# Block 2's odd steps: the weight split behind the gate banks and the lag rows

## What is computed

```
h = rms_norm(x, norm_gain[layer])
proj = h @ w_in[layer]
q, k, v, z_a, u, z_s, g_a, g_s = jnp.split(proj, SPLITS, axis=-1)
y_a = band_attention(heads(q), heads(k), heads(v), rel_bias[layer])
y_a = (y_a * jax.nn.silu(z_a)) @ w_attn_out[layer]
y_s = s5_ssm(u, ...)
y_s = jax.nn.gelu(y_s)
glu_a, glu_b = jnp.split(y_s @ w_glu[layer] + b_glu[layer], 2, axis=-1)
y_s = glu_a * jax.nn.sigmoid(glu_b)
y_s = (y_s * jax.nn.silu(z_s)) @ w_ssm_out[layer]
merged = jax.nn.sigmoid(g_a) * y_a + jax.nn.sigmoid(g_s) * y_s
x = x + merged @ w_out[layer]
```

## Time and profile before

| | |
|---|---|
| median of the runs | 1469.31 us |
| profiled execution, its own time | 1469.46 us |
| its span in the profile | 1467.6 us |
| granted TensorE clock, mean | 0.999 |
| TensorE busy | 1374.2 us (94%) |
| VectorE busy | 546.7 us (37%) |
| ScalarE busy | 339.7 us (23%) |
| GpSimd busy | 115.3 us (8%) |

### The profile page before, as it was taken

One profiled execution on the slowest core, in us unless ns is written; L12 is line 12 of the kernel. 1 busy time (PEld: TensorE's weight loads), 2 busy tenths in 40 slices (PEclk: granted clock), 3 DMA queues, 4 the chain that ended last, 5 costly groups with the idle time before them and its releaser, 6 DMA issues.

```text
span 1467.6 us, 16657 instructions
## 1 busy us (share of the span) xinstructions
PE 1374.2 (94%) x6713; PEld 737.4 (50%) x6713; DVE 546.7 (37%) x965; ACT 339.7 (23%) x549; POOL 115.3 (8%) x190
## 2 busy tenths in 40 slices
PE   7999999999998898998988988989899999999997
PEld 6778433333333232332332323324378787888876
DVE  7675621121211121121111211213268587756663
ACT  5893110010000000010000000103042465533322
POOL 0000000000000000000000000002022214550000
PEclk9999999999999999999999999999999999999999
DMA  9149899999999999999999999999975133253231
GB/s 324 22 172 385 324 420 406 428 427 428 429 429 430 429 430 430 429 429 429 430 429 429 429 429 428 428 428 428 404 245 139 58 101 86 83 171 134 92 110 58
DMA packets 67827, 467.31 MB, mean 318 GB/s; under 512 B 5760, under 2 KB 30592, under 8 KB 42688
## 3 DMA queue, kind: packets, MB, share of 16 engines
q1 hardware_dynamic: 62864, 454.71, 75.4%
q0 software_dynamic: 4624, 11.44, 3.1%
q10 hardware_dynamic: 288, 0.45, 0.1%
HBM read 458.49 MB, written 7.05 MB: 317 GB/s over the span
## 4 chain that ended last, share of the span: by engine, by line
PE 62%; DMA 30%; DVE 4%; ACT 2%; issue 2%; DVEq 0%; POOL 0%; ACTq 0%
DMA wide<-in_w_up 22%; PE bank L1028 13%; PE bank L970 12%; PE bank L724 8%; PE bank L726 8%; PE bank L725 8%; DMA early<-in_w_up 8%; PE bank L911 4%; PE bank L998 1%; PE bank L1066 1%; DVE nrm L1746 1%; PE bank L1125 1%; PE bank L1153 1%; PE bank L754 1%; PE bank L764 0%
## 5 line engine op out<-in xcount | busy, mean ns | idle before, releaser
L970 PE MATMUL bank<-wide,xinT 128*64 128x512 f32 x1376 | 307.2, 596 | 43.2 <-DMA wide<-in_w_up 24.6
L970 PEld LDWEIGHTS bank<-wide,xinT 128*64 128x64 f32 x1376 | 96.5, 137 | 249.7 <-issue 170.5
L970 PE MATMUL bank<-early,xinT 128*64 128x512 f32 x656 | 147.2, 596 | 19.8 <-DMA early<-in_w_up 11.1
L1746 DVE SCALAR_TENSOR_TENSOR th<-th,bank 128x512 f32<-128x512 f32 x32 | 20.6, 684 | 387.8 <-ACT th L1451 387.8
L1028 PE MATMUL bank<-wide,actT 128*64 128x512 f32 x656 | 145.1, 595 | 3.6 <-issue 3.4
L724 PE MATMUL bank<-hT_lo,ring_r 128*128 128x512 f32 x352 | 138.6, 394 | 1.4 <-ACT gt L1316 1.1
L726 PE MATMUL bank<-hT_hi,ring_r 128*128 128x512 f32 x352 | 137.1, 389 | 0.0
L725 PE MATMUL bank<-hT_hi,ring_r 128*128 128x512 f32 x352 | 137.0, 389 | 0.0
L1451 ACT ACTIVATE th<-bank 128x512 f32<-128x512 f32 x32 | 17.4, 595 | 477.1 <-PE bank L970 477.1
L1743 DVE TENSOR_TENSOR ring_r<-ring,ring_r 128x2048 fp32r<-128x2048 f32 (+1 forms) x40 | 89.4, 2236 | 59.9 <-ACT ring_r L1284 59.4
L970 PEld LDWEIGHTS bank<-early,xinT 128*64 128x64 f32 x656 | 45.9, 137 | 119.2 <-issue 79.1
(11 more groups left out here) (427 smaller groups left out, 1705.4 us busy)
## 6 DMA issues: line engine op xcount, KB each, us to landing
wide<-in_w_gate SPq DMA_DIRECT2D x43, 2048.0 KB, 37.7
wide<-in_w_up SPq DMA_DIRECT2D x42, 2048.0 KB, 39.0
wide<-in_w_down SPq DMA_DIRECT2D x39, 2048.0 KB, 38.5
early<-in_w_down SPq DMA_DIRECT2D x21, 2048.0 KB, 38.5
early<-in_w_up SPq DMA_DIRECT2D x21, 2048.0 KB, 39.0
early<-in_w_gate SPq DMA_DIRECT2D x20, 2048.0 KB, 40.1
ring<-in_w_in SPq DMA_DIRECT2D x25, 1024.0 KB, 6.2
ring<-in_w_out SPq DMA_DIRECT2D x8, 1024.0 KB, 4.9
```

The source lines that it names most:

```text
L970: last = pe.matmul(bank[1 + 2 * (m % 2) + q // 2][o:o + 64, :], xinT[:, k, :], w[:, i, q * 512:(q + 1) * 512], start=(k == 0), stop=(k == ...
L1746: return dve.scalar_tensor_tensor(out_, a, s, b, op0, op1)
```

## The change

In the odd steps 1, 3, 5 and 7 VectorE calls `weights_lo(M + 9 + i)` behind the gates' evictions and the lag rows instead of ahead of them. Nothing is added or removed, and the programs of the other engines are the same.

```diff
                 if i % 2 == 1 and i < HEADS:
                     states(i // 2)
-                weights_lo(M + 9 + i)
+                late = i % 2 == 1 and i < HEADS
+                if not late:
+                    weights_lo(M + 9 + i)
                 if i == HEADS:
...
-                if i % 2 == 1 and i < HEADS:
+                if late:
                     c = i // 2
                     lag_rows(c)
+                    weights_lo(M + 9 + i)
                     if c + 1 < CT:
                         full(dve, f"st_im_{c}")
                         input_table(c + 1)
```

## The result

The changed kernel takes 1477.23 us (median of 6 runs, 1476.0 to 1478.43) against 1469.73 us for the kernel before (6 runs). The ratio is 1.0051, with a 95% interval of 1.0038 to 1.0064: slower by 7.5 us. The forecast was 1473.9 us, with a range to 1475.5. The direction was right; of the 7.5 us the forecast's sum had 4.6.

The account below looks back on a forecast made before the run. TensorE's products were taken to bound block 2, so other engines count only where TensorE waits. Terms -0.84 + 0.58 + 1.49 + 1.68 + 1.67 = +4.58 us gave 1473.9 us, range 1472.0 to 1475.5.

Parts of the forecast that it names:

- The wait in step 3 goes, -0.84: TensorE's wait before step 3's lag product, for a gate bank VectorE has not yet emptied, goes whole: -0.84 us.
- Room of 1.8 us for the split in steps 1, 3 and 5, 0.58 us too little in step 7: The later weight split is ready 1.8 us early in three odd steps; behind step 7 TensorE waits for it: +0.58 us.
- What stands behind the split is late by 2.21 us: VectorE's lateness passes through ScalarE's state copies to TensorE's state products in steps 2, 4, 6: +1.49, +1.68, +1.67 us.
- DMA queues: no term: SP's loads shift with the units TensorE has used; GpSimd's store and Toeplitz loads don't stand behind the split: no cost.
- Rivals 1, 2 and 3: Lateness caught up, 1469.1 us (chance 0.07); partly caught up, 1471.2 (0.07); removed wait worth over 2.94 us (0.01).
- rival 4: New TensorE stands lower its clock to 1.2 GHz behind the three stalls: up to 11 us each, up to 1507; chance 0.01.
- longer hand-overs: Upper bound of the range: four hand-overs could each be 0.4 us longer than the 0.14 taken, 1.6 us in all.

Follow-up runs that it names:

- The moved copies: Changed kernel with ScalarE's two state table copies put ahead of the two gates' tanh in steps 2, 4 and 6: 1471.36 us, ratio 1.0013.
- unread passes: Changed kernel plus two TensorE passes whose result is never read, before the state products of steps 2, 4 and 6: 1474.78 us, ratio 1.0033.

## Why the prediction was right and wrong

- *The wait in step 3 goes, -0.84.* Right: it goes with the split moved in step 3 alone.
- *Room of 1.8 us for the split in steps 1, 3 and 5, 0.58 us too little in step 7.* Right: there is no wait in the first three and one of 0.50 us in the last.
- *What stands behind the split is late by 2.21 us, ScalarE passes it on in full, and it is paid in each of steps 2, 4 and 6.* Right, with 5.03 us for a forecast 4.84. The moved copies took 3.2 us of it away.
- *DMA queues: no term.* Nothing speaks against it: the waits and the clock leave 0.1 us over.
- *Rivals 1, 2 and 3*, that the lateness is caught up in full or in part, or that the removed wait is worth more: none of it happened.
- **The step that failed is the clock, put at nothing in the sum.** Its fall was rival 4, with a chance of 0.01, on the ground that waits of up to 1.7 us for weight loads stand in the trace, that all slices of the span read 9 or more and that the projections of step 3 ran at 1.00. Those waits show that a wait of that length need not take the clock down, not that it can't; and a slice of 37 us doesn't show a fall of some 3 us, since the page of the changed kernel, with two falls, has a 9 in all 40 slices as well. The price was off as well: 11 us for each fall assumed that the clock stays down through two projections, and it came back after some 3 us, so that a fall costs 1.4 to 1.5. Two falls, 2.9 us, were missing from the sum in the profiled run, and the range's upper bound did not allow for them: the 1.6 us above the forecast were for longer hand-overs.
- *Whether the parts add up.* The kernel with only step 1 moved shows that the stall of step 2 alone removes the 0.84 us, as does moving the split in step 3. The same 0.84 us can be had only once, and the forecast counted it once. The waits of the four single kernels make 0.7 + 0.9 + 1.8 + 0.5 = 3.8 us (less the 0.84 twice), those of the changed kernel 4.7: the waits add up if the 0.84 is taken off once. The measured differences make 0.25 + 1.0 + 3.6 + 0.1 = 4.9 us against 7.5; without the one fall seen there and the two here it is 3.4 against 4.6.

## What to carry to other kernels

A wait that is removed by moving work back on an in-order engine has to be set against the lateness of all that now stands behind it: follow that lateness through the next engines to the first product that has less spare time than it. A new idle stretch on TensorE costs its own length and, in some executions, a stretch at the lower clock around or behind it: here 1.4 to 1.5 us for each. Price both, and look for such a fall in slices of a microsecond, not of 37. Where the engine must wait, see whether useful work can lie in the wait. Profile such a kernel more than once, since one profile shows only the falls of one execution.

## What the runs showed of the hardware that was not expected

**Behind equal waits the clock fell in some executions and not in others.** Steps 2, 4 and 6 had the same waits in three profiled executions of one program, and the clock fell in steps 2 and 6, in step 4, and in none. Together with the kernels that move one split, twelve waits of 1.5 to 1.8 us were profiled, and the clock fell at four of them. With the idle time cut to at most 0.4 us by unread passes, or to 0.6 by earlier copies, none of ten waits in four profiled executions had a fall. What decides between executions was not found, nor whether the chip has a part in it.

**VectorE's states take less time when they start later.** In step 3 of the kernel before, GpSimd builds its next table while VectorE computes the states. The first operation of that table, and VectorE's timeline there:

```profile
1211.40 1.05 POOL L1693 TENSOR_TENSOR wc<-pw_re,bc 128x512 f32<-128x512 f32 x1 [12.90 <-PE bank L1202]
```

```profile
1212.45 0.42 DVE L1743 TENSOR_TENSOR tmp<-bank,rotc 128x256 f32<-128x256 f32 x1 [2.18 <-PE bank L1187]
...
1213.90 2.45 DVE L1743 TENSOR_TENSOR tmp<-tmp 128x256 f32<-128x256 f32 x2
1216.38 1.03 DVE L2243 TENSOR_TENSOR_SCAN tmp<-mag,tmp 128x64 f32<-128x64 f32 x1
...
1217.52 1.31 DVE L2243 TENSOR_TENSOR_SCAN tmp<-mag,tmp 128x64 f32<-128x64 f32 x1
```

The same in the kernel with only step 1 moved, where the state product comes 1.5 us later against TensorE's other work and GpSimd's table does not:

```profile
1210.86 1.05 POOL L1693 TENSOR_TENSOR wc<-pw_re,bc 128x512 f32<-128x512 f32 x1 [12.89 <-PE bank L1202]
```

```profile
1213.49 0.42 DVE L1743 TENSOR_TENSOR tmp<-bank,rotc 128x256 f32<-128x256 f32 x1 [1.57 <-PE bank L1187]
...
1214.94 1.99 DVE L1743 TENSOR_TENSOR tmp<-tmp 128x256 f32<-128x256 f32 x2
1216.97 1.27 DVE L2243 TENSOR_TENSOR_SCAN tmp<-mag,tmp 128x64 f32<-128x64 f32 x1
...
1223.30 2.29 DVE L1743 TENSOR_TENSOR ring_r<-ring,ring_r 128x2048 fp32r<-128x2048 f32 x1
```

From the first operation to the split it is 1223.50 - 1212.45 = 11.05 us before and 1223.30 - 1213.49 = 9.81 us here, 1.2 less. In step 1 of the kernel before, where GpSimd computes no table, it is 1186.54 - 1179.37 = 7.17; the pair of additions there:

```profile
1180.81 0.76 DVE L1743 TENSOR_TENSOR tmp<-tmp 128x256 f32<-128x256 f32 x2
```

So the stall of step 2 gave the gate's eviction in step 3 the time that it lacked. The Trainium skill (SBUF — State Buffer, Who interferes with whom) has it that a VectorE instruction with two SBUF inputs contends with a GpSimd instruction that reads SBUF; the rows agree, since the pair of additions takes 2.45 us beside the table and 0.76 us in step 1, and the products that read a bank and a table keep their 0.42 us. By that rule the wait in step 3 of the kernel before would at bottom be one for GpSimd's table: the states take 3.9 us longer there than in step 1, and the wait is 0.84 us. This is argued and not shown, since no run here moved that table by itself.
